# Moving the weight halves by 16 to 224 bytes in a partition, stage by stage

## The chip, the cores and the metric

The kernel runs on one core of a Trainium2 chip. The metric is the device time of one execution in microseconds. The times beside it come from repeated executions; the profile is of one further execution, taken by the hardware profiler. Lower is better.

## What is computed

The reference is a stack of transformer-like layers on 512 latent tokens (and, in the first layer, 256 context tokens) of width 1024, in fp32:

```python
for i in range(DEPTH):          # layer 0 "even", layer 1 "odd"
    x = x + gate1 * mixer(modulate(rms_norm(x, g1), shift1, scale1))
    x = x + gate2 * squared_relu_mlp(modulate(rms_norm(x, g2), shift2, scale2), w1, w2)
# mixer of layer 0: p = h @ w_in; a depthwise convolution of one half, differential attention
#   of the other, joined and multiplied by w_out
# mixer of layer 1: p = h @ w_in; long convolutions of one half, a gated delta rule of the other, w_out
# then two second layers: attention with latents and a gated recurrence beside it, both projected,
#   joined, multiplied by w_out, then a gated MLP (w_gate, w_up, w_down)
```

Most of the arithmetic is in the products `h @ w`. Everything else is norms, gates, convolutions, attention and scans between them.

## The kernel before

Each stage's products are run by one helper, `products` (lines 189 to 539). Activations stand with their features on the 128 partitions and tokens along the free axis. So that a product of fp32 numbers is precise in the chip's faster fp32r format, each operand is split into a **high half** (the fp32r rounding) and a **low half** (the rest), and each pair of blocks costs three matmuls: weight high by activation high, weight high by activation low, weight low by activation high (line 519 issues them all, in this order). The stationary operand, which TensorE loads ahead of each matmul, is a 128x128 block of a weight half; the moving operand is 512 latent tokens or 256 context tokens of an activation half. Three matmuls for each of the 128-row blocks of the weights add up in one PSUM bank. In jobs with `rows` the operands change places: a block of activations is stationary, and 512 columns of a weight half move. Jobs marked `native` are plain fp32 products without halves, and so are those of lines other than 519.

The weights of one unit (as a rule 8 blocks of 128 rows by 128 columns, or 4 by 256: 1024 numbers in each partition) pass through three stations:

- SP loads the unit from HBM into one of three or four buffers `raw`.
- VectorE makes the high half by a copy with a cast (`halve_weights`, line 356), into one of three buffers `high`.
- GpSimd makes the low half by a subtraction (`lower_weights`, line 450), into one of three buffers `low`.
- TensorE waits for the low half of the unit (line 450's semaphore) and issues its matmuls. A buffer of `high` and `low` comes free when the matmuls of the unit three before are done.

Buffers are stacked: each is allocated where the one before it ended, at the next multiple of 32 bytes in the partition. In `products` the order is `raw`, `low`, `high`, each of 12,288 bytes (16,384 for a `raw` of four). The halves of the activations were allocated by the caller before them. So the distance in a partition from an activation half to a weight half follows from the sizes of what lies between. All blocks of halves are multiples of 512 bytes apart, and all buffers between them are multiples of 512 bytes, with two exceptions:

- In the odd layer's input products the buffer `pads` (2 by 776 numbers, 6,208 bytes, that is 12 times 512 plus 64) lies between the halves and `raw`.
- In the second layers `lb`, `last`, `columns` and `marks` (32, 64, 96 and 48 bytes, the last one rounded up to 64: 256 together) lie between the part `work`, in which the halves named `x_high`, `ya_high` and `yb_high` are placed, and the halves of the normed input; after these come the weights.

In this text the **offset** of a stage is the distance from its activation halves to its weight halves, modulo 512 bytes. In the kernel before it is 0 in the even layer's four stages of products listed below, in the odd layer's output product and in its MLP; 64 in the odd layer's input products; and in the second layers 0 for the products of the normed input and the MLP's down product, and 256 for those of `x_high`, `ya_high`, `yb_high`.

The stages, in order of time, with the matmuls of halves in each:

| stage | function | matmuls of 512 columns | of 256 columns |
|---|---|---|---|
| even input | `even_mixer` | 528 | 384 |
| even output | `even_output` | 192 | 192 |
| even MLP | `squared_relu_mlp` (latent and context) | 1536 | 1536 |
| odd input | `odd_projections` | 696 | 216 |
| odd output | `odd_layer` | 192 | 0 |
| odd MLP | `squared_relu_mlp` (latent alone: `own_room`) | 1536 | 0 |
| second layers, each of two passes | `layer_products` | 2880 | 0 |

The counts follow from the strips of the jobs, 8 to 32 blocks of rows in each, and three matmuls for each block. In the second layers the first third of a stage has attention, scans and native products between the matmuls of halves; the later part (output, gate, up and down products) is almost nothing but them.

Of the kernel before, what the change touches and what calls it, by code (L numbers as in the profile page):

```python
# [188 lines left out]
def products(nc, m, jobs, ring_tiles=RING, beside=None, beside_scalar=None, signals=(), with_signals=None,  # L189
             before=None, loads=(), sides=(), banks=8, sums=None, settled=False):  # L190

# [69 lines left out]
    with ExitStack() as held:  # L261
        raw, low, high = held.enter_context(buffers(nc, raw=[P, R, 1024], low=([P, RH, 1024], F32R),
                                                    high=([P, RH, 1024], F32R)))
        block, *sems = held.enter_context(stage(
            nc, *[f"weights_loaded{r}" for r in range(R)], "high_ready", "low_ready", "accumulated",
# [1468 lines left out]
def squared_relu_mlp(nc, m, x, w1, w2, toks, scale, shift, gate, sides=()):  # L1734
# [5 lines left out]
    with ExitStack() as held:  # L1740
        *h, hid = held.enter_context(buffers(nc, **pair, hid=[P, FF1 // P, width]))
        room = held.enter_context(buffers(nc, **pair)) if own_room else h
        before = Norm(m, x, hid[:, 0:DC, :], hid[:, DC, :], DC, toks, D, scale, shift, halves=h, given=True)

        def relu(act, c, s, y):
            t0, tn = toks[s]
            return act.activation(hid[:, c, t0:t0 + tn], y, ACT.Relu)  # L1747

        def square(dve, c, s):
            t0, tn = toks[s]  # L1750
            return dve.tensor_tensor(hid[:, c, t0:t0 + tn], hid[:, c, t0:t0 + tn], hid[:, c, t0:t0 + tn], ALU.mult)  # L1751

        products(nc, m, [Job(w1, strip(0, FF1), h, toks, relu, "scalar", square),
                         Job(w2, FULL, hid, toks, residual(x, gate)(toks), "vector", written_by=0, room=room,
                             lead=6 if own_room else 1, room_after=None if own_room else 0)],
                 ring_tiles=3, before=before, sides=sides, sums=SquareSums(m, x, toks))

# [64 lines left out]
def even_mixer(nc, m, A, x, mods, small, gain, mix, q, k, v, written):  # L1822
# [4 lines left out]
    with ExitStack():  # L1827
        scale = lambda c, s: gain[:, c, s:s + 1]
        with ExitStack():
            w_in = A["ev_w_in"][0, :, :]  # L1830
            with ExitStack():
                with buffers(nc, conv=[P, 4, TG]) as conv:
                    with buffers(nc, pad=[P, 4, TG + GAP], odd_taps=[P, TG], flat=[P, 2, 512],
# [42 lines left out]
                        def convolve(dve, u, stored, signals):  # L1876
# [3 lines left out]
                            for c, n in steps[(u - 2) * per_unit:(u - 1) * per_unit] if 2 <= u <= last_unit else []:  # L1880
# [16 lines left out]
                                else:  # L1897
# [11 lines left out]
                                 beside=convolve, signals=("convolved",), with_signals=convolution_signals, before=before,  # L1909
                                 ring_tiles=3, banks=6, sides=[copies, Modulation(  # L1910
                                     m, A, [(0, n) for n in range(4, 12)],
# [15 lines left out]
def even_output(nc, m, A, x, mods, small, gain, mix):  # L1927
    toks = (LAT, CTX)
    shift = lambda which: (lambda c, s: mods[:, which * DC + c, s:s + 1])
    with buffers(nc, high=([P, DC, TA], F32R), low=([P, DC, TA], F32R)) as halves:  # L1930
        products(nc, m, [Job(A["ev_w_out"][0, :, :], FULL, mix, toks, residual(x, shift(2))(toks), "vector",
                             room=halves)],
                 ring_tiles=3, sides=[Gain(gain, mods, small.norm_g[:, 1, :], 4)], sums=SquareSums(m, x, toks))

# [797 lines left out]
def odd_layer(nc, m, A, x, mods, small, gain, spectra):  # L2732
# [5 lines left out]
    with buffers(nc, mix=[P, DC, T], u=[P, 12, T], gate=[P, 4, T]) as (mix, u, gate):  # L2738
# [9 lines left out]
        with buffers(nc, high=([P, DC, T], F32R), low=([P, DC, T], F32R)) as halves:  # L2748
            products(nc, m, [Job(A["od_w_out"][0, :, :], FULL, mix, (LAT,),
                                 residual(x, shift(2))((LAT,)), "vector", room=halves)],  # L2750
                     sides=[Gain(gain, mods, small.norm_g[:, 3, :], 4)], sums=SquareSums(m, x, (LAT,)))
    squared_relu_mlp(nc, m, x, A["mlp_w1"][1, :, :], A["mlp_w2"][1, :, :], (LAT,), scale, shift(3), shift(5))
# [57 lines left out]
def odd_projections(nc, m, w_in, halves, before, pads, short_w, short_b, conv_w, u, qk, v, gate, rest, squares, roots):  # L2810
# [45 lines left out]
    def convolve(dve, unit, stored, signals):  # L2856
# [16 lines left out]
        beside=convolve, signals=("convolved",), with_signals=with_signals, before=before,  # L2873
        ring_tiles=3, banks=7, sides=[delta])

# [945 lines left out]
def layer_products(nc, m, A, l, x, columns, halves, latent_halves, state_halves, x_halves, part, q, f, gate, i_rows,  # L3821
# [60 lines left out]
    def gated(dst, n):  # L3882
        def take(dve, c, s, y):
# [40 lines left out]
            written_by=15, room=halves, room_after=13, lead=6)],  # L3924
        before=before, ring_tiles=3, settled=True, sides=[constants, prep, attention, forget, levels, gates, states, norm], sums=SquareSums(m, x, toks))

# [121 lines left out]
```

How the kernel before makes its waits and increments, by code:

```python
    def __call__(self, ins):  # L54
        self.mark(ins)
        self.eng.wait_ge(self.sem, self.n)
# [6 lines left out]
    def wait(self, n=None):  # L63
        n = self.n if n is None else n
        if n > 0:
            self.eng.wait_ge(self.sem, n)
# [60 lines left out]
        @block.scalar  # L127
        def _(act):
            for dst, src in pairs[1::2]:
                act.dma_start(dst, src, allow_slow_non_contiguous=True).then_inc(arrived, 16)
            act.wait_ge(arrived, 16 * len(pairs))
# [2 lines left out]
def issue(eng, pairs, arrived):  # L135
    for dst, src in pairs:
        eng.dma_start(dst, src, allow_slow_non_contiguous=True).then_inc(arrived, 16)
    eng.wait_ge(arrived, 16 * len(pairs))
# [49 lines left out]
def products(nc, m, jobs, ring_tiles=RING, beside=None, beside_scalar=None, signals=(), with_signals=None,  # L189
# [127 lines left out]
        def stored(eng, j, c, part):  # L317
            p = index[j, c, part]
            if p in follow_at:
                eng.wait_ge(followed[follow_at[p][0]], follow_at[p][1])
            else:
                eng.wait_ge(taken[taken_at[p][0]], taken_at[p][1])
# [4 lines left out]
            j = len(jobs) - 1  # L327
            ended = {c: max(u for u, (i, cs, _, _) in enumerate(units) if i == j and c in cs)
                     for c in range(len(jobs[j].chunks))}
            first = min(c for c in ended if bank_of[index[j, c, 0]] == 0 and ended[c] >= len(units) - 4)
            sums.follow(raw, j, jobs[j].parts, ended, first, len(units),
                        lambda eng: eng.wait_ge(low_ready, halved(len(units) - 1)))
        @block.sync
```

## Time and profile before

| | |
|---|---|
| median of the runs shown | 3940.62 us (3938.89 to 3942.35) |
| span of the profiled execution, first to last instruction | 3934.4 us |
| TensorE matmuls, busy | 3645.1 us, 93% of the span, 18,494 instructions |
| TensorE weight loads, busy | 2932.7 us, 75% |
| VectorE, ScalarE, GpSimd, busy | 2035.1, 864.5, 1369.6 us |
| mean granted TensorE clock | 0.962 of full speed |

A time of an execution is some 5 to 8 us longer than the span, which begins with the first instruction and ends with the last; no separate time of the profiled execution is given. The recorded duration of a matmul holds its way through the array, so records overlap and "busy" counts the overlap once; the distance from one start to the next is what a matmul costs in a stream. In a timeline the first column is the start in us, the second the duration in us; "x16" means that 16 instructions of one form were merged into one line, and its duration runs to the end of the last. In a view of windows each engine has its busy time and the number of its instructions.

### The profile page before, as it was taken

The numbers are of one execution on the slowest core, as the hardware profiler recorded it, in microseconds if no ns is written. First come the engines' busy times: TensorE is split into PE (matmuls) and PEld (weight loads), VectorE is DVE, ScalarE is ACT, GpSimd is POOL, SyncE is SP. The second block draws the span as 40 slices with busy tenths as digits, with TensorE's granted clock in tenths as the row PEclk, the third lists the DMA queues.
The fourth block names the chain that finished last, engine by engine and source line by source line (L and its number), as shares of the span: only waits on it lengthen the run. The fifth ranks groups of instructions, "written<-read, shape, count | busy, mean of one in ns | idle before, by whom it ended". The sixth has DMA issues, their size and how long they took to land. (4 is left out here: it accounts for less than half of the span.)

```text
span 3934.4 us, 45661 instructions
## 1 busy us (share of the span) xinstructions
PE 3645.1 (93%) x18494; PEld 2932.7 (75%) x18494; DVE 2035.1 (52%) x3169; ACT 864.5 (22%) x1690; POOL 1369.6 (35%) x599
## 2 busy tenths in 40 slices
PE   6898988999989999968999899799999898899998
PEld 3684567888877889857888566688888576788887
DVE  5797643224446457673233367864243377853342
ACT  3213512110011233301100344422000344421001
POOL 2331043225554200005455222235455222245454
PEclk9898989999999999989999899999999999999999
DMA  5443312221113100112322232123332222223322
GB/s 171 150 150 134 129 43 75 60 64 59 61 53 91 51 1 1 51 45 73 98 94 91 61 81 53 50 67 100 97 92 80 82 61 54 52 78 96 97 91 80
DMA packets 400349, 306.78 MB, mean 78 GB/s; under 512 B 11228, under 2 KB 367782, under 8 KB 399559
## 3 DMA queue, kind: packets, MB, share of 16 engines
q1 hardware_dynamic: 398040, 303.37, 25.5%
q8 instruction: 149, 2.44, 0.3%
q10 hardware_dynamic: 2095, 0.44, 0.1%
q14 instruction: 65, 0.53, 0.0%
HBM read 297.48 MB, written 6.29 MB: 77 GB/s over the span
## 5 line engine op out<-in xcount | busy, mean ns | idle before, releaser
L450 POOL TENSOR_TENSOR low<-raw,high 128x1024 fp32r<-128x1024 f32 (+1 forms) x437 | 1049.5, 2402 | 2090.4 <-DVE high L356 2090.4
L519 PE MATMUL scores<-high 128*128 128x512 f32 (+1 forms) x1944 | 741.5, 381 | 72.0 <-DVE low L704 32.4
L519 PE MATMUL scores<-low,high 128*128 128x512 f32 (+1 forms) x1944 | 727.1, 374 | 0.0
L519 PE MATMUL scores<-high,low 128*128 128x512 f32 (+1 forms) x1944 | 726.3, 374 | 0.0
L356 DVE CAST high<-raw 128x1024 fp32r<-128x1024 f32 (+1 forms) x437 | 397.5, 910 | 499.6 <-PE scores L519 257.7
L519 PE MATMUL bank<-high 128*128 128x512 f32 (+1 forms) x1480 | 541.5, 366 | 0.2
L519 PE MATMUL bank<-low,high 128*128 128x512 f32 (+1 forms) x1480 | 538.8, 364 | 0.0
L519 PE MATMUL bank<-high,low 128*128 128x512 f32 (+1 forms) x1480 | 538.1, 364 | 0.0
L519 PEld LDWEIGHTS scores<-high 128*128 128x128 f32 x1944 | 375.5, 193 | 154.2 <-POOL low L450 53.9
L519 PEld LDWEIGHTS scores<-high,low 128*128 128x128 f32 x1944 | 374.6, 193 | 65.5
L519 PEld LDWEIGHTS scores<-low,high 128*128 128x128 f32 x1944 | 376.2, 194 | 61.7 <-issue 1.0
L519 PEld LDWEIGHTS bank<-high 128*128 128x128 f32 x1480 | 279.3, 189 | 49.3 <-issue 4.9
L519 PEld LDWEIGHTS bank<-high,low 128*128 128x128 f32 x1480 | 279.0, 189 | 45.1
L519 PEld LDWEIGHTS bank<-low,high 128*128 128x128 f32 x1480 | 279.3, 189 | 44.1 <-issue 0.5
L752 ACT ACTIVATE raw<-x_all 128x512 f32<-128x512 f32 (+1 forms) x48 | 32.4, 700 | 1070.3 <-POOL low L450 1013.7
L1751 DVE TENSOR_TENSOR hid<-hid 128x512 f32<-128x512 f32 x96 | 60.8, 633 | 328.5 <-ACT hid L1747 328.5
L519 PE MATMUL bank<-x_high,high 128*128 128x512 f32 x448 | 174.3, 389 | 0.0
L519 PE MATMUL bank<-x_low,high 128*128 128x512 f32 x448 | 174.3, 389 | 0.0
L519 PE MATMUL bank<-x_high,low 128*128 128x512 f32 x448 | 174.3, 389 | 0.0
L398 POOL TENSOR_TENSOR low<-hid,high 128x1536 fp32r<-128x1536 f32 (+1 forms) x23 | 103.7, 4509 | 132.7 <-DVE high L387 132.7
L519 PE MATMUL scores<-x_high,high 128*128 128x512 f32 x256 | 100.0, 391 | 0.0
L519 PE MATMUL scores<-x_high,low 128*128 128x512 f32 x256 | 99.6, 389 | 0.0
(632 smaller groups left out, 5260.2 us busy)
## 6 DMA issues: line engine op xcount, KB each, us to landing
raw<-in_mlp_w SPq DMA_DIRECT2D x128, 512.0 KB, 3.9
raw<-in_w_in SPq DMA_DIRECT2D x76, 512.0 KB, 3.9
ring<-in_ada_w SPq DMA_DIRECT2D x32, 1024.0 KB, 7.1
raw<-in_w_gate SPq DMA_DIRECT2D x44, 512.0 KB, 3.8
raw<-in_w_up SPq DMA_DIRECT2D x44, 512.0 KB, 3.8
raw<-in_w_down SPq DMA_DIRECT2D x40, 512.0 KB, 3.4
mix<-in_ada_w SPq DMA_DIRECT2D x16, 1024.0 KB, 6.3
raw<-in_od_w_in SPq DMA_DIRECT2D x29, 512.0 KB, 3.9
```

The costliest lines, as they stand in the source:

```text
L356: dve.tensor_copy(tile(high, u), tile(raw, u)).then_inc(high_ready, 1)
L398: return eng.tensor_tensor(low_, act, high, ALU.subtract)
L450: pool.tensor_tensor(tile(low, u), tile(raw, u), tile(high, u).bitcast(F32), ALU.subtract)\
L519: mm = pe.matmul(out(p), stationary, moving, start=(k0 + k == 0 and i == 0), stop=(k0 + k == job.kc - 1 and i == len(pairs) - 1))
L752: act.activation(self.tile(c), self.x[:, c, 0:self.width], ACT.Square).then_inc(self.squared, 1)
L1751: return dve.tensor_tensor(hid[:, c, t0:t0 + tn], hid[:, c, t0:t0 + tn], hid[:, c, t0:t0 + tn], ALU.mult)
```

## The change

`products` gets a parameter `skew`. `low` is allocated larger by that many 4-byte numbers and used from `skew` numbers on; `high`, which is allocated behind it, begins so much later too, rounded up to 32 bytes. No instruction is added or taken away, and `raw`, the activations and the order of the work stay as they are.

```diff
@@ products
-             before=None, loads=(), sides=(), banks=8, sums=None, settled=False):
+             before=None, loads=(), sides=(), banks=8, sums=None, settled=False, skew=0):
...
-        raw, low, high = held.enter_context(buffers(nc, raw=[P, R, 1024], low=([P, RH, 1024], F32R),
+        raw, low, high = held.enter_context(buffers(nc, raw=[P, R, 1024], low=([P, RH * 1024 + skew], F32R),
                                                     high=([P, RH, 1024], F32R)))
+        low = low[:, skew:].rearrange("p (r n) -> p r n", r=RH)
@@ squared_relu_mlp
-                 ring_tiles=3, before=before, sides=sides, sums=SquareSums(m, x, toks))
+                 ring_tiles=3, before=before, sides=sides, sums=SquareSums(m, x, toks), skew=32 if own_room else 4)
@@ even_mixer
-                                 ring_tiles=3, banks=6, sides=[copies, Modulation(
+                                 ring_tiles=3, banks=6, skew=48, sides=[copies, Modulation(
@@ even_output
-                 ring_tiles=3, sides=[Gain(gain, mods, small.norm_g[:, 1, :], 4)], sums=SquareSums(m, x, toks))
+                 ring_tiles=3, sides=[Gain(gain, mods, small.norm_g[:, 1, :], 4)], sums=SquareSums(m, x, toks), skew=56)
@@ odd_layer
-                     sides=[Gain(gain, mods, small.norm_g[:, 3, :], 4)], sums=SquareSums(m, x, (LAT,)))
+                     sides=[Gain(gain, mods, small.norm_g[:, 3, :], 4)], sums=SquareSums(m, x, (LAT,)), skew=12)
@@ odd_projections
-        ring_tiles=3, banks=7, sides=[delta])
+        ring_tiles=3, banks=7, skew=24, sides=[delta])
@@ layer_products
-        before=before, ring_tiles=3, settled=True, sides=[constants, prep, attention, forget, levels, gates, states, norm], sums=SquareSums(m, x, toks))
+        before=before, ring_tiles=3, settled=True, skew=24, sides=[constants, prep, attention, forget, levels, gates, states, norm], sums=SquareSums(m, x, toks))
```

The offsets become:

| stage | skew in bytes | offset before | offset after, of low / of high |
|---|---|---|---|
| even input | 192 | 0 | 192 |
| even output | 224 | 0 | 224 |
| even MLP | 16 | 0 | 16 / 32 |
| odd input | 96 | 64 | 160 |
| odd output | 48 | 0 | 48 / 64 |
| odd MLP | 128 | 0 | 128 |
| second layers | 96 | 0 and 256 | 96 and 352 |

## Rows read from the trace of the kernel before

**Rows 1.** The page, part 1: busy time (share of the span) and instructions.

```profile
PE 3645.1 (93%) x18494; PEld 2932.7 (75%) x18494; DVE 2035.1 (52%) x3169; ACT 864.5 (22%) x1690; POOL 1369.6 (35%) x599
```

**Rows 2.** Windows by stage, line 519 alone: window, length, PE, PEld, clock, DMA, GB/s.

```profile
121.70:321.60 199.90, 174.28 (x912) 147.99 (x912) 0.98 0.41 129
525.30:594.40 69.10, 68.97 (x384) 60.38 (x384) 0.97 0.12 39
605.40:1154.10 548.70, 541.42 (x3072) 475.89 (x3072) 0.99 0.20 59
1167.10:1371.00 203.90, 195.31 (x912) 158.20 (x912) 0.98 0.24 68
...
1820.70:2177.80 357.10, 354.46 (x1536) 291.71 (x1536) 0.98 0.30 90
2204.60:2590.00 385.40, 262.28 (x1016) 194.37 (x1016) 0.97 0.23 61
2590.00:3050.20 460.20, 442.09 (x1944) 364.42 (x1944) 1.00 0.29 88
```

**Rows 3.** Timeline of PE, odd MLP (offset 0): 55 matmuls, first and last.

```profile
1999.65 0.39 PE L519 MATMUL bank<-low,high 128*128 128x512 f32 x1
...
2011.89 0.39 PE L519 MATMUL scores<-low,high 128*128 128x512 f32 x1
```

**Rows 4.** Timeline of PE, even MLP (offset 0): ten matmuls of 256 columns, then 512.

```profile
1010.50 0.28 PE L519 MATMUL scores<-high,low 128*128 128x256 f32 x1
...
1011.70 0.40 PE L519 MATMUL bank<-high 128*128 128x512 f32 x1
1011.94 0.40 PE L519 MATMUL bank<-low,high 128*128 128x512 f32 x1
1012.17 0.39 PE L519 MATMUL bank<-high,low 128*128 128x512 f32 x1
1012.40 0.40 PE L519 MATMUL bank<-high 128*128 128x512 f32 x1
1012.63 0.39 PE L519 MATMUL bank<-low,high 128*128 128x512 f32 x1
1012.86 0.39 PE L519 MATMUL bank<-high,low 128*128 128x512 f32 x1
```

**Rows 5.** Timeline of PE, odd input (offset 64): 512 columns, ten matmuls in all.

```profile
1221.70 0.39 PE L519 MATMUL scores<-low,high 128*128 128x512 f32 x1
1221.93 0.40 PE L519 MATMUL scores<-high,low 128*128 128x512 f32 x1
1222.17 0.39 PE L519 MATMUL scores<-high 128*128 128x512 f32 x1
1222.40 0.40 PE L519 MATMUL scores<-low,high 128*128 128x512 f32 x1
...
1223.80 0.40 PE L519 MATMUL scores<-low,high 128*128 128x512 f32 x1
```

**Rows 6.** Timeline of PE, odd input (offset 64): 256 columns, thirteen matmuls, first and last.

```profile
1290.28 0.28 PE L519 MATMUL scores<-high,low 128*128 128x256 f32 x1
...
1291.64 0.28 PE L519 MATMUL scores<-high,low 128*128 128x256 f32 x1
```

**Rows 7.** Timeline of PE: native fp32 products of 512 columns, second layer.

```profile
2267.96 3.60 PE L519 MATMUL bank<-raw,work 128*128 128x512 f32 x8
2271.39 7.03 PE L519 MATMUL scores<-raw,work 128*128 128x512 f32 x16
```

**Rows 8.** Timeline of PE: halves, 512 columns, at half the granted clock; seven matmuls.

```profile
2205.63 0.63 PE L519 MATMUL scores<-high,low 128*128 128x512 f32 x1
...
2208.19 0.61 PE L519 MATMUL scores<-high,low 128*128 128x512 f32 x1
```

**Rows 9.** Groups by line, 2600 to 3040 us: the two engines that make the halves.

```profile
L450 POOL TENSOR_TENSOR low<-raw,high 128x1024 fp32r<-128x1024 f32 (+1 forms) x79 | 186.2, 2358 | 186.7 <-DVE high L356 186.7
...
L356 DVE CAST high<-raw 128x1024 fp32r<-128x1024 f32 (+1 forms) x79 | 68.5, 868 | 86.6 <-PE scores L519 50.8 <-PE bank L519 35.8
```

## The prediction

> **What bounds the kernel now.** I read the page's busy times first, then line 519 by windows of one stage each, then single starts in the timeline, and last the engines that feed TensorE. TensorE's matmuls are busy for 3645 of 3934 us [rows 1]. The windows show where: the products of halves fill their stages almost without a gap, 541 of 549 us in the even MLP, 354 of 357 in the odd MLP, 442 of 460 in the later part of a second layer; only in that layer's first part is line 519 busy for less, 262 of 385 us [rows 2]. The second pass of the second layers repeats the last two windows, with the same 1016 and 1944 instructions (80 of the 1016 are native passes, which leaves 936 matmuls of halves). So the time goes as the distance from one matmul's start to the next, and an edit matters as far as it changes that distance.
>
> The distance is the reading on which all else rests. In the odd MLP 54 steps take 12.24 us, 226.7 ns each [rows 3]. At the full clock of 2.4 GHz 512 columns are 213.3 ns, so 13.3 ns of each step are something else. In the even MLP the matmuls of 256 columns lie 120.0 ns apart (1.20 us for ten), again 13.3 ns over their 106.7 [rows 4]. The odd input stage runs the same instructions on the same shapes with the full clock, and its steps differ: 512 columns take 2.10 us for nine, 233.3 ns [rows 5], and 256 columns 1.36 us for twelve, 113.3 ns [rows 6]. The kernel's text names one thing in which this stage stands apart: its offset is 64 and not 0 or 256. So the offset matters, in both directions: it adds 6.7 ns to 512 columns and takes 6.7 ns from 256.
>
> Two more readings say what the extra is. Native fp32 products, which pass their columns at half the rate, lie 3.43 us / 8 = 428.8 ns apart [rows 7]; and halves at the half clock of 1.2 GHz lie 2.56 us / 6 = 426.7 ns apart, which is 512 columns and nothing more [rows 8]. Where the moving operand is read at half speed, the extra is 0 to 2.1 ns. It comes up when the moving read runs at its full rate beside the load of the next weights, and I take it for the two reads getting in each other's way in SBUF, which the offset shifts against each other. It also depends on when they start: after the 256-column matmuls the 512-column ones begin with steps of 240, 230, 230, 230 and 230 ns as printed [rows 4], longer than the 226.7 of a long run [rows 3]. The settled steps are 113.3, 120.0, 226.7 and 233.3 ns, all multiples of 6.67 ns. I expect other offsets to settle on this ladder too.
>
> **A rule on this.** The step of the same instruction on the same shape is 226.7 ns at offset 0 and 233.3 at 64 [rows 3, 5]. The Trainium skill, "TensorE: Matmul & The Clock Gate", section "Step-by-step: what each phase is for", says that TensorE reads SBUF through two independent ports and that loading the next weights takes no read bandwidth from the running matmul; "SBUF — State Buffer", section "SBUF: two separate sides", lets only VectorE and GpSimd contend on the engine side. By that rule an offset changes nothing and the time stays where it is; the trace disagrees by the 6.7 ns above. The same page on TensorE puts a warm step of 512 columns at 215.7 ns; if all steps fell to that, the sum would be about 130 us below the time before, an estimate from that page. No run here shows such a step for halves.
>
> **What the change removes, adds and moves.** It adds and removes no instruction, wait or transfer. It moves where three streams touch SBUF: VectorE's cast writes `high`, GpSimd's subtraction reads `high` and writes `low`, and TensorE reads both.
>
> *VectorE and GpSimd:* I cost them at nothing. A unit of 1024 weights feeds 24 matmuls of 512 columns, 24 x 226.7 ns = 5.44 us, while its cast takes 0.87 us and its subtraction 2.36 us [rows 9]. Both could take twice as long and the unit would still be ready in time; at 220 ns a step the unit takes 5.28 us, which changes nothing. The cover would go only if the subtraction took over 5.3 us.
>
> *TensorE, bounds.* The new offsets (192, 224, 16/32, 160, 48/64, 128, 96/352) stand in no row, so I bound the step. Below: 213.3 + 2.1 = 215.4 ns for 512 columns and 106.7 + 2.1 = 108.8 for 256, if the extra falls to that of the native products [rows 7]. Above: 512 columns at 240 ns, the longer of the two steps that alternate at offset 64 as they are printed, to 10 ns [rows 5], and 256 at 120 as now.
>
> *TensorE, what I take.* The value nearest to the rows is one rung of the ladder up, none, or one down, by stage. At offset 0 both reads begin in the same place of every 256 bytes; taking that away was worth a rung to 256 columns, whose whole length lies beside a load, and cost a rung at 64 to 512 columns. I let offsets that are no multiple of 64 go one rung down, 64-like ones behave as the odd input does, and 128 change nothing, being as symmetric as 0 and 256:
>
> - second layers, later part, two passes: 2 x 1944 x 6.67 ns = -25.9 us;
> - second layers, first part: 2 x 936 x 6.67 = 12.5; line 519 stands back behind other work there (262 of 385 us busy [rows 2]), so I let half of it arrive: -6.2;
> - even MLP: (1536 + 1536) x 6.67 = 20.5; its shift of 16 and 32 bytes is at most half the 64 of the odd input, so half: -10.2;
> - even output: (192 + 192) x 6.67 = -2.6;
> - odd input, leaving 64: 696 x 6.67 = -4.6, its 256 columns unchanged;
> - even input, 192 being 64 short of 256: +528 x 6.67 - 384 x 6.67 = +1.0;
> - odd MLP and odd output: 0.
>
> The sum is -48.5 us. For the profiled execution that is a span of 3934.4 - 48.5 = 3885.9; the median of the runs, 3940.6, is 6.2 us above that execution's span, and with it I forecast 3892 us, 1.2% less. Nothing new is late after that: GpSimd has half of each unit free, and DMA moves at 0.2 to 0.4 of its share in these windows [rows 2].
>
> **Rivals.**
>
> *The collisions go away almost everywhere.* Every stage settles at least one rung lower, at best at 215.4 and 108.8 ns. For: with the reads at half speed the extra is already gone, so it is no fixed cost [rows 7, 8]. Against: no settled step of halves in the trace is under 226.7 ns for 512 columns. One rung everywhere: 512 columns 2 x 1944 + 936 (half of the two first parts) + 1536 + 192 + 192 + 1536 + 696 + 528 = 9504, 256 columns 1536 + 192 + 384 = 2112; 11,616 x 6.67 ns = 77 us, 3863 us. At the lower bound: (9504 - 696) x 11.3 + 696 x 17.9 + 2112 x 11.2 + 216 x 4.5 ns = 137 us, 3804 us.
>
> *The new offsets are like 64, and the kernel gets slower.* The mechanism is the one seen in the odd input: away from 0, steps of 512 columns settle a rung higher and those of 256 a rung lower. For: it is the only offset other than 0 and 256 that the trace has, and 512 columns are four fifths of the matmuls. Against: one point says little of seven others. Price: (9504 - 696) x 6.67 - 2112 x 6.67 = +45 us, 3985 us. It decides as soon as the second layers go up, which hold half of these 512-column steps; with 240 ns everywhere and 256 columns unchanged it would be 8808 x 13.3 = +117, 4058 us.
>
> *Nothing happens.* Either the steps depend on something else that sets the odd input stage apart, or the gains and losses by stage cancel: 3941 us. For: 256 and 0 give the same step although they are different places. Against: rows 5 and 6 beside rows 3 and 4. That the change doesn't do what it says belongs here too: the offset would have to be undone by the allocation, and the sizes leave no room for that.
>
> **How the numbers follow.** I give the forecast (some stages a rung down, 3862 to 3925) 0.42, the collisions going away almost everywhere 0.23, nothing 0.15, slower 0.20. The predicted time is the forecast's, 3892 us. The range reaches from the lower bound of the second case to the price of the third, in round numbers 3805 to 3990 us. A measurement of this kernel tells about 2% (79 us) from no change: below 3862 lies nearly all of the second case and a part of the forecast, 0.30; above 4019 only the far end of the slower case, 0.07; the rest is 0.63.
>
> **What would show it.** In the timeline of the changed kernel the settled step of each stage tells: 220 ns in the second layers' later part and in the even output would show the forecast's main terms right, 226.7 would show that the offset doesn't matter there, 233 or more the slower rival. The odd input at 226.7 or less would show that 64 was its trouble. 226.7 in the odd MLP would show that 128 counts as 0. The number of instructions, the durations of the cast and the subtraction, and the DMA must be as before. I'm wrong if the second layers' step goes up, or if steps under 216 ns appear.

## The result and the profile after

The changed kernel takes 3990.12 us (median of 3989.98 and 3990.26) beside 3940.62 before: 1.0124 times as long, with an interval of 1.0095 to 1.0154. The forecast was 3892 us, 1.2% faster. The span of the profiled execution grew from 3934.4 to 3988.1 us, by 53.7. In every run for which both are given an execution takes 2.1 to 2.2 us more than its span (here 3990.26 and 3988.1), and not 5 to 8 as the section on the time before has it. So the profiled execution of before took some 3936.6 us, 4 us under its median, and the spans differ by more than the medians, which are 49.5 us apart. What came about is the second rival, "the new offsets are like 64, and the kernel gets slower", priced at 3985 us.

Page, part 1, of the kernel after, answering to [rows 1]:

```profile
PE 3705.6 (93%) x18494; PEld 2942.7 (74%) x18494; DVE 2031.9 (51%) x3169; ACT 864.1 (22%) x1690; POOL 1371.4 (34%) x599
```

Every count is the same, and VectorE, ScalarE and GpSimd are busy as long as before to within 4 us. TensorE's matmuls are busy for 60.5 us longer, its weight loads for 10.0.

Windows by stage of the kernel after, answering to [rows 2] with the same columns (the helper's line is 520 now):

```profile
122.50:323.10 200.60, 173.83 (x912) 146.40 (x912) 0.98 0.41 129
524.10:593.70 69.60, 69.50 (x384) 60.14 (x384) 0.97 0.13 38
605.10:1161.30 556.20, 548.04 (x3072) 475.90 (x3072) 0.99 0.19 58
1174.20:1379.40 205.20, 197.04 (x912) 160.23 (x912) 0.98 0.24 67
1774.10:1820.30 46.20, 46.20 (x192) 37.23 (x192) 0.96 0.16 49
1830.80:2195.50 364.70, 361.82 (x1536) 291.91 (x1536) 0.99 0.30 88
2221.50:2606.90 385.40, 265.09 (x1003) 193.43 (x1004) 0.96 0.23 60
2606.90:3085.90 479.00, 459.93 (x1958) 368.58 (x1956) 1.00 0.28 86
```

No stage became shorter. The even MLP went from 548.7 to 556.2 us, the odd MLP from 357.1 to 364.7; the last two windows, a whole pass of the second layers, from 845.6 to 864.4. The granted clock of each window is the one it had, to 0.01, and a weight load of line 519 or 520 lasts 0.19 us on average in both kernels: the growth is neither a lower clock nor a longer load.

The step, the distance between two starts, shows where it lies. First second layers, then odd MLP (answering to [rows 3]), in the timeline of PE of the kernel after:

```profile
2899.69 0.40 PE L520 MATMUL bank<-x_low,high 128*128 128x512 f32 x1
...
2904.14 0.40 PE L520 MATMUL bank<-x_high,low 128*128 128x512 f32 x1
...
1999.70 0.40 PE L520 MATMUL bank<-low,high 128*128 128x512 f32 x1
...
2004.82 0.40 PE L520 MATMUL bank<-high,low 128*128 128x512 f32 x1
```

The first two rows span 19 steps in 4.45 us, 234.2 ns each; the last two 22 steps in 5.12 us, 232.7 ns. In these rows the moving operand's half comes first, then the weights': "low,high" is the activations' low half by the weights' high one. Before, the odd MLP had 226.7 [rows 3], and so had the second layers, in the timeline of PE of the kernel before:

```profile
2899.27 0.39 PE L519 MATMUL bank<-x_low,high 128*128 128x512 f32 x1
...
2902.67 0.39 PE L519 MATMUL bank<-x_low,high 128*128 128x512 f32 x1
```

These are 15 steps in 3.40 us.

Two answers to [rows 8] and [rows 7], halves at half the clock and native products, in the timeline of PE of the kernel after:

```profile
2222.10 0.63 PE L520 MATMUL scores<-low,high 128*128 128x512 f32 x1
...
2224.23 0.63 PE L520 MATMUL scores<-high 128*128 128x512 f32 x1
...
2287.14 3.60 PE L520 MATMUL bank<-raw,work 128*128 128x512 f32 x8
```

Five steps in 2.13 us are 426 ns, as before. Over all steps of 512 columns at the half clock each stage of both kernels has a mean of 426.6 to 426.9 ns, so the distance shows in the step only at the full 2.4 GHz. Eight native products last 3.60 us, as before, but that says nothing of the distance: the change moved neither `raw` nor `work`. The engines that make the halves, groups from 2617 to 3057 us of the kernel after, answer to [rows 9]:

```profile
L451 POOL TENSOR_TENSOR low<-raw,high 128x1024 fp32r<-128x1024 f32 x76 | 182.4, 2401 | 196.6 <-DVE high L357 196.6
...
L357 DVE CAST high<-raw 128x1024 fp32r<-128x1024 f32 x76 | 68.0, 895 | 72.1 <-PE scores L520 42.1 <-PE bank L520 30.0
```

A unit's cast takes 0.90 us and its subtraction 2.40, of the 24 x 234.2 ns = 5.62 us in which TensorE uses the unit up: they stay covered.

By stage, from its first to its last matmul of halves; the steps are means over all that follow each other without a gap at the full clock, before and after:

| stage | us before, after | predicted, measured | step of 512 columns, ns | step of 256 columns, ns |
|---|---|---|---|---|
| even input | 199.5, 200.2 | +1.0, +0.7 | 227.8 to 230.3 | 119.7 to 116.7 |
| even output | 68.7, 69.2 | -2.6, +0.5 | 229.0 to 233.1 | 119.4 to 117.4 |
| even MLP | 548.3, 555.8 | -10.2, +7.5 | 228.4 to 232.9 | 119.5 to 119.0 |
| odd input | 203.5, 204.8 | -4.6, +1.3 | 233.3 to 233.3 | 113.6 to 119.9 |
| odd output | 45.0, 45.9 | 0, +0.9 | 226.7 to 231.2 | |
| odd MLP | 356.6, 364.4 | 0, +7.8 | 226.7 to 232.4 | |
| second layers, pass 1 | 845.1, 863.9 | -16.1, +18.8 | 227.2 to 234.2 | |
| second layers, pass 2 | 845.6, 864.3 | -16.1, +18.7 | 227.1 to 234.2 | |

The measured terms add up to +56.2 us, the span to +53.7; the stretches between the stages gave back 2.5.

### The profile page after: what moved, and what is told of

Same layout as the page of the kernel before. It is cut to its first block and busy times, and to the rows that moved or that the text cites. A ratio compares the mean times of both kernels' runs of the same rounds, so it can differ in the third digit from the quotient of the medians.

```text
span 3988.1 us, 45661 instructions
## 1 busy us (share of the span) xinstructions
PE 3705.6 (93%) x18494; PEld 2942.7 (74%) x18494; DVE 2031.9 (51%) x3169; ACT 864.1 (22%) x1690; POOL 1371.4 (34%) x599
## 5 line engine op out<-in xcount | busy, mean ns | idle before, releaser
L520 PE MATMUL scores<-high 128*128 128x512 f32 (+1 forms) x1944 | 751.1, 386 | 71.6 <-DVE low L705 30.8
L520 PE MATMUL scores<-low,high 128*128 128x512 f32 (+1 forms) x1944 | 737.1, 379 | 0.0
L520 PE MATMUL scores<-high,low 128*128 128x512 f32 (+1 forms) x1944 | 734.7, 378 | 0.0
L520 PE MATMUL bank<-high 128*128 128x512 f32 (+1 forms) x1480 | 547.2, 370 | 0.2
```

The source lines that it names most:

```text
L520: mm = pe.matmul(out(p), stationary, moving, start=(k0 + k == 0 and i == 0), stop=(k0 + k == job.kc - 1 and i == len(pairs) - 1))
```

## The experiments

All compute the whole of the reference. Diffs are against the changed kernel, shortened to the arguments and lines that differ, and "without `skew`" means that the argument is taken out. Where only one run was made, it is read by its stages, which say more here than its time; the time of the kernel before on the same chip stands beside each, since chips differ by some us.

**1. Everything at a distance of 0 or 256.** The even input and second layers get a distance of 256, the odd input 64 + 192 = 256. In the odd MLP and the two output products, activations and weights move together by 96 bytes; the even MLP is as before.

```diff
@@ squared_relu_mlp
+        if own_room:
+            held.enter_context(buffers(nc, gap=[P, 24]))
-  skew=32 if own_room else 4
@@ even_mixer, layer_products
-  skew=48
+  skew=64
...
-  skew=24
+  skew=64
@@ odd_projections
-  skew=24
+  skew=48
@@ even_output, odd_layer
-    with buffers(nc, high=
+    with buffers(nc, gap=[P, 24]), buffers(nc, high=
...
-  skew=56
...
-  skew=12
```

> Every stage has offset 0 or 256, but not the places of before: even input and second layers move their weights by 256 bytes, the odd input by 192 (offset 256 in place of 64), and in the even output, odd MLP and odd output activations and weights move together by 96 bytes. The even MLP is unchanged. Theory (the distance between weight halves and activation halves modulo 256 sets the step): 226.7 ns in all these stages, in the odd input too, where 512 columns fall from 233.3 to 226.7 (696 x 6.67 = -4.6 us) and 256 columns rise from 113.3 to 120 (216 x 6.67 = +1.4 us); the sum is 3937 us. Rival A (the place of the weights in the partition itself, or any move, sets it): the second layers at 230 to 235 ns and the odd MLP at 231 to 233, 3970 to 3995 us. Rival B (the engines that write the halves are slowed by a new place): the odd MLP as in the changed kernel, and longer casts or subtractions.

Measured: 3932.36 us (median of 10) beside 3935.53 (13), a ratio of 0.9994 with an interval of 0.9984 to 1.0003. In the timeline of PE of this kernel, odd input (answering to [rows 5]), then odd MLP:

```profile
1221.71 0.39 PE L520 MATMUL scores<-high 128*128 128x512 f32 x1
...
1225.79 0.39 PE L520 MATMUL scores<-high 128*128 128x512 f32 x1
...
1999.75 0.39 PE L520 MATMUL bank<-low,high 128*128 128x512 f32 x1
...
2003.15 0.39 PE L520 MATMUL scores<-low,high 128*128 128x512 f32 x1
```

Eighteen steps in 4.08 us and fifteen in 3.40 are 226.7 ns each. So the odd input was not a stage with slow products: it had a bad distance, and at 256 its 512 columns fall from 233.3 to 227.2 on average, its 256 columns rise from 113.6 to 119.7, and the stage takes 200.8 us, not 203.5. In the odd MLP, moving both operands together by 96 bytes changed nothing. With the parameter still there and the distances at 0 or 256, the whole growth is gone. In the places tried it is the distance of the two that counts, modulo 256, and not the place of either.

**2. The low weight halves alone.** They begin where the change puts them; the high halves stay where they were modulo 256, at 64 in the odd input and at 0 elsewhere. The even MLP is as before.

```diff
@@ products
+        room = skew + (-skew) % 64
-  low=([P, RH * 1024 + skew], F32R)
+  low=([P, RH * 1024 + room], F32R)
-        low = low[:, skew:].rearrange("p (r n) -> p r n", r=RH)
+        low = low[:, skew:skew + RH * 1024].rearrange("p (r n) -> p r n", r=RH)
@@ squared_relu_mlp
-  skew=32 if own_room else 4
+  skew=32 if own_room else 0
```

> Only the low weight halves move, by the amounts of the change; the high halves begin at offset 0 again (64 and 0 as before in the odd input's case: it moves by 256), and the even MLP is as before. Theory (the loads of the weights meet the moving reads): two loads of three stay aligned, so the settled sequence is broken but less often disturbed: second layers between 228 and 233 ns, odd MLP likewise, 3950 to 3980 us. Rival A (the place of the high halves alone decides): 226.7 ns, 3940 us. Rival B (GpSimd's writing of the low halves at the new place is what costs): the whole price of the change without the even MLP's 7 us, 234 ns in the second layers, 3982 us.

Measured: 3976.84 us (before on this chip 3935.53). The second layers take 859.2 and 860.1 us at a mean step of 232.5 ns, the odd MLP 361.9 at 231.1. The timeline of PE of this kernel, odd MLP:

```profile
2000.14 0.39 PE L521 MATMUL bank<-high 128*128 128x512 f32 x1
2000.37 0.40 PE L521 MATMUL bank<-low,high 128*128 128x512 f32 x1
2000.60 0.40 PE L521 MATMUL bank<-high,low 128*128 128x512 f32 x1
2000.84 0.39 PE L521 MATMUL bank<-high 128*128 128x512 f32 x1
2001.06 0.40 PE L521 MATMUL bank<-low,high 128*128 128x512 f32 x1
...
2003.61 0.39 PE L521 MATMUL bank<-high 128*128 128x512 f32 x1
```

Fifteen steps in 3.47 us, 231.3 ns: a triple of unequal steps that repeats. Averaged over the stage, the step after "high" is 226.7 ns, that after "low,high" 232.5, that after "high,low" 234.2. Only the last two have the moved low weights beside them: the second while they are loaded for the next matmul, the third while the matmul itself uses them. Here two thirds of the steps carry the whole loss. The second layers of the same run, with the low weights at 96, don't follow that: the step after "high", which has no moved weights beside it, is the longest there, 233.2 ns, that after "low,high" 231.7 and that after "high,low" 232.6. Moving one weight half alone doesn't help in either, and a single step isn't explained by the operands beside it alone.

**3 and 4. Other distances.** Each stage gets another skew, so that a distance is seen in more than one stage (the numbers of the diffs are of 4 bytes).

```diff
@@ even_mixer: skew
-  48
+  16, and 8 in the fourth
@@ even_output
-  56
+  32, and 40
@@ squared_relu_mlp, odd and even
-  32 and 4
+  16 and 16, and 48 and 8
@@ odd_projections
-  24
+  8, and 56
@@ odd_layer
-  12
+  24, and 8
@@ layer_products
-  24
+  8, and 40
```

> Other offsets by stage: even input 64, even output 128, even MLP 64, odd input 96, odd output 96, odd MLP 64, second layers 32. Theory (the offset modulo 256 alone decides, whatever the stage): odd MLP 233.3 ns as the odd input had at 64, even MLP 512 columns at 233 and 256 columns at 113.3, odd input at 96 the 234 ns that the second layers had there; the second layers at 32 are unknown, 227 to 236. Sum for 230 ns at 32: 3975 us. Rival A (each stage has its own best place, by what lies around it): the odd MLP at 64 differs from 233.3 by over 2 ns, and the even MLP's 256 columns stay at 119 to 120.

> Even input 32, even output 160, even MLP 32 for both halves, odd input 32 (288), odd output 32, odd MLP 192, second layers 160. Theory (offset alone): the second layers at 160 show the odd input's 233.3 ns of the changed kernel, the odd output and input at 32 the step of the second layers in the run with 32 there, the odd MLP at 192 near the even input's 230 or above; no stage under 226.7 ns, 3975 to 4000 us. Rival (a better place exists): one of the offsets 32, 160, 192 gives 220 ns or less for 512 columns; in the second layers that would be 3905 us or less.

Measured: 3974.29 and 3976.83 us (before on this chip 3935.53). The timeline of PE of the third kernel: even MLP at 64, 256 columns and then 512, and odd MLP at 64.

```profile
699.86 0.28 PE L520 MATMUL bank<-high 128*128 128x256 f32 x1
...
700.54 0.39 PE L520 MATMUL bank<-high 128*128 128x512 f32 x1
...
2000.07 0.39 PE L520 MATMUL bank<-high 128*128 128x512 f32 x1
...
2003.57 0.39 PE L520 MATMUL bank<-high 128*128 128x512 f32 x1
```

Six steps of 256 columns in 0.68 us are 113.3 ns, and fifteen of 512 in 3.50 us are 233.3: what [rows 6] and [rows 5] showed of 64 in the odd input, now in two other stages. The stage is no cause; the distance is. And in the fourth kernel's odd MLP, at 192, in its timeline of PE:

```profile
1999.61 0.39 PE L520 MATMUL bank<-low,high 128*128 128x512 f32 x1
...
2003.73 0.39 PE L520 MATMUL bank<-low,high 128*128 128x512 f32 x1
```

Eighteen steps in 4.12 us, 228.9 ns, under the 230 that was expected from the even input (why is told below the table of distances), the least away from 0 in these two kernels. None comes below 226.7. As a whole the even MLP at 64 was no longer than before, 547.7 us beside 548.3 to 549.6 in the runs that left it at 0: what its 512 columns lost, its 256 columns gave back.

**5 and 6. Small distances.** Both weight halves get 64 numbers more room and are used from `skew` on, so that distances of a few bytes can be set.

```diff
@@ products
+        low_room = (RH * 1024 + 64 if skew else RH * 1024)
-  low=([P, RH * 1024 + skew], F32R), high=([P, RH, 1024], F32R)
+  low=([P, low_room], F32R), high=([P, low_room], F32R)
-        low = low[:, skew:].rearrange("p (r n) -> p r n", r=RH)
+        low, high = (t[:, skew:skew + RH * 1024].rearrange("p (r n) -> p r n", r=RH) for t in (low, high))
```

> Offsets of few bytes to either side of 0 (both weight halves at the same one): even input 248, even output 252, odd input 240, odd output 8, odd MLP 4, second layers 16; even MLP unchanged. Theory (the two reads of TensorE meet, and 0 is a place where the sequence settles at 226.7): the step rises off 0 as it did at 32, to between 228 and 235 ns; 3950 to 3985 us. Rival (0 is an accident of a grid of 32 bytes, and a better place lies a few bytes off): 220 ns or less in the second layers at 16 or in the odd MLP at 4, 3905 us or less. Third possibility (lines of 16 bytes or more are read whole, so that less than a line makes no difference): 226.7 at 4, 8, 248 and 252.

> The same with other amounts: even input 240, even output 232, odd input 112, odd output 24, odd MLP 16, second layers 8. Theory: the odd MLP at 16 repeats the second layers of the run beside it within 1 ns, the even input at 240 its odd input; the second layers at 8 lie between 226.7 and the step at 16; 3945 to 3985 us. Rival (a better place a few bytes off): 220 ns or less somewhere.

Measured: 3954.22 and 3953.92 us (before on this chip 3939.88). Four bytes are enough: the odd MLP went from 226.7 to 232.4 ns. That rules out the third possibility, by which less than 16 bytes would change nothing. The expectation that one distance gives one step fell at 16 bytes: 229.1 ns on average in the second layers of the fifth kernel, 233.3 in the odd MLP of the sixth. The timeline of PE of the fifth kernel, second layers, shows why:

```profile
2699.67 0.39 PE L521 MATMUL bank<-high,low 128*128 128x512 f32 x1
...
2702.47 0.39 PE L521 MATMUL scores<-x_high,low 128*128 128x512 f32 x1
...
2799.62 0.39 PE L521 MATMUL bank<-x_low,high 128*128 128x512 f32 x1
...
2803.02 0.39 PE L521 MATMUL scores<-x_low,high 128*128 128x512 f32 x1
```

Twelve steps in 2.80 us are 233.3 ns; 97 us later, in the same stage and at the same distance, fifteen in 3.40 are 226.7. Taken by streaks without a gap, of at least a dozen steps, 3443 of the 5426 steps lie in streaks with a mean of 227 ns, 1807 in streaks of 233, and 176, all in the job with `rows`, between. A streak keeps its level until it is interrupted. So 16 bytes have two settled levels, and the distance alone doesn't decide which is taken; the mean of a stage hides that.

All distances, with the mean step in ns (of several stages where there are two numbers; the stages of 512 columns alone give the cleaner ones):

| bytes, modulo 256 | 512 columns | 256 columns |
|---|---|---|
| 0 | 226.7 to 229.0 | 119.4 to 119.7 |
| 4, 8 | 232.4, 230.7 | |
| 16 | 229.1 (of streaks at 227 and 233) and 233.3 | |
| 24, 32 | 231.1, 233.0 to 233.3 | 118.3 to 118.7 (at 32) |
| 64 | 232.1 to 233.3 | 113.5 to 113.7 |
| 96, 112 | 234.2, 233.3 | 117.5, 119.8 |
| 128 | 232.4 to 233.5 | 118.2 |
| 160 | 233.2 to 233.4 | 119.9 to 120.1 |
| 192 | 228.9 to 230.3 | 116.7 |
| 224, 232 | 233.1, 231.1 | 117.4, 118.4 |
| 240, 248, 252 | 227.5 to 230.5, 233.1, 233.3 | 118.2 to 119.2, 117.8, 120.0 |

The even input's means of 512 columns mix two kinds of job. In its last 144 matmuls, a job with `rows`, the weights move and the activations are stationary, so the distance from the moving operand to the stationary one is the offset with the other sign: 64 where the table says 192, and 192 where it says 64. The timeline of PE shows it: the changed kernel (192), first an ordinary job, then the one with `rows`, and the latter in the third kernel (64):

```profile
148.04 0.39 PE L520 MATMUL bank<-high 128*128 128x512 f32 x1
...
153.31 0.39 PE L520 MATMUL bank<-high,low 128*128 128x512 f32 x1
...
293.99 0.40 PE L520 MATMUL scores<-high,low 128*128 128x512 f32 x1
...
301.69 0.39 PE L520 MATMUL scores<-high,low 128*128 128x512 f32 x1
...
292.69 0.39 PE L520 MATMUL scores<-high 128*128 128x512 f32 x1
...
297.73 0.39 PE L520 MATMUL scores<-low,high 128*128 128x512 f32 x1
```

These are 23 steps in 5.27 us, 229.1 ns; 33 in 7.70, 233.3; and 22 in 5.04, 229.1. So at 192 and 64 the step goes by the distance from the moving to the stationary operand, with its sign: the ordinary jobs have the 228.9 of the odd MLP at 192, the job with `rows` the 233.3 of 64. At 16 and 240 the mirror fails: with an offset of 240 the ordinary jobs have 228.3, within 1 ns of the odd input's 227.5 as expected, but the job with `rows` 236.4, which is no level of 16, and the second layers' job with `rows` at 16 has 231.2 to 231.8.

**7. Each length at its better place.** 512 columns are shortest at 0 and 256 columns at 64, so the context tokens' halves get buffers of their own, 64 bytes further from the weights than a multiple of 256, while the latent ones are at 0 (or 256). This is done in the even input, the first product of the even MLP and the odd input; all else is without `skew`.

```diff
+class Apart:
+    def __init__(self, latent, context):
+        self.latent, self.context = latent, context
+    def __getitem__(self, key):
+        p, c, t = key
+        return self.context[p, c, t.start - T:t.stop - T] if t.start >= T else self.latent[p, c, t]
+APART = dict(context_high=([P, DC, TC], F32R), context_low=([P, DC, TC], F32R), gap=[P, 16],
+             latent_high=([P, DC, T], F32R), latent_low=([P, DC, T], F32R))
...
@@ odd_projections
-  skew=24
+  skew=48
```

> The weights stay at offset 0 to the latent tokens' activations, and in three stages the context tokens' activations alone are put 64 bytes off: their halves get buffers of their own, 64 bytes ahead of the place that would be 0 (even input, the first job of the even MLP, odd input). The odd input's weights move by 192 bytes, so that its 512 columns come to 256. Everything else is at the places of before. Theory (each matmul's step follows from the distance of its moving operand to the weights that are loaded beside it): 512 columns stay at 227 to 229 ns, and 256 columns fall from 120 to 113.3 in the even input (384 x 6.3 = -2.4 us) and the even MLP's first half (768 x 6.2 = -4.7 us) and stay at 113.3 in the odd input, whose 512 columns fall to 227 (-4.2 us): -11 us together, ratio 0.997. Rival (a stage has one state for all its columns, and a 64 in it spoils the settled sequence of 512): 512 columns at 230 to 233 ns in these stages, and the sum no better than before, ratio 1.000 or above.

Measured: 3930.94 us (median of 11) beside 3939.39 (15) for the kernel before, a ratio of 0.998 with an interval of 0.9971 to 0.9989: a small gain, but over both kernels. The timeline of PE of this kernel, even MLP, from 256 to 512 columns:

```profile
699.72 0.28 PE L520 MATMUL bank<-context_high,low 128*128 128x256 f32 x1
...
700.90 0.39 PE L520 MATMUL bank<-latent_high,high 128*128 128x512 f32 x1
701.13 0.39 PE L520 MATMUL bank<-latent_low,high 128*128 128x512 f32 x1
701.35 0.39 PE L520 MATMUL bank<-latent_high,low 128*128 128x512 f32 x1
...
703.85 0.39 PE L520 MATMUL bank<-latent_low,high 128*128 128x512 f32 x1
```

Ten steps of 256 columns take 1.18 us, 118.0 ns, and thirteen of 512 take 2.95, 226.9. The even input takes 198.9 us (199.5 before), the even MLP 547.2 (548.3), the odd input 200.4 (203.5); 3.1 of these 4.8 us are the odd input's, whose 512 columns leave 64. The rest of the 8.4 us between the medians is not located; these two traces are of different chips. The 256 columns came to 118 and not to the 113.3 that I had expected from experiment 3: I had taken 64 to set their step by itself, and it doesn't where both distances are in one stage. The rival, by which the 64 would have spoilt the 512 columns, didn't come about either: they stay at 226.9. The cause of the 118 stays open, and by the stages 4.8 us came of the 11 that were expected. The second product of the even MLP and the even output were not taken apart.

**8. The second layers undone.** The changed kernel, without `skew` in the second layers alone.

```diff
@@ layer_products
-  skew=24
```

> The changed kernel with the second layers' weights back at their place of before; the other stages keep the change. Theory (the price is a sum of independent stages, and the second layers hold most of it): their two passes go back from 864 to 845.5 us each, 3990 - 37 = 3953 us, with the other stages' steps as in the changed kernel. Rival (the price comes from somewhere else and is only seen there): more than 10 us away from 3953.

Measured: 3958.89 us (before on this chip 3939.39). The passes are back at 846.0 and 846.2 us. The other stages of the table above sum to +18.7, which makes 3958.1: the terms of the stages add. One step is not as in the changed kernel, though. In the odd output, where the two kernels are the same, the timeline of PE shows the changed kernel's first and then this one's:

```profile
1777.64 0.40 PE L520 MATMUL scores<-high,low 128*128 128x512 f32 x1
...
1819.94 0.40 PE L520 MATMUL bank<-high,low 128*128 128x512 f32 x1
...
1780.88 0.39 PE L520 MATMUL scores<-high,low 128*128 128x512 f32 x1
...
1823.57 0.40 PE L520 MATMUL bank<-high,low 128*128 128x512 f32 x1
```

183 steps without a gap take 42.30 and 42.69 us, 231.2 and 233.3 ns. So 16 bytes are not the only distance with more than one level: at 48 and 64 the same code kept one of two in two executions.

**9. One activation half, or one weight half, moved.** In the odd MLP the low activation halves alone are moved, by 128 bytes; in the second layers the high weight halves alone, by 128; in the odd output the low activation halves by 64; all else is without `skew`.

```diff
@@ products
-        low = low[:, skew:].rearrange("p (r n) -> p r n", r=RH)
+        low = low[:, 0:RH * 1024].rearrange("p (r n) -> p r n", r=RH)
@@ squared_relu_mlp
+        if own_room:
+            pair = dict(high=pair["high"], gap=[P, 32], low=pair["low"], rest=[P, 32])
...
+            h, room = h[0::2], room[0::2]
@@ odd_layer
-        with buffers(nc, high=([P, DC, T], F32R), low=([P, DC, T], F32R)) as halves:
+        with buffers(nc, high=([P, DC, T], F32R), gap=[P, 16], low=([P, DC, T], F32R), rest=[P, 48]) as (*halves,):
+            halves = halves[0::2]
@@ layer_products
-  skew=24
+  skew=32
```

> Each group of three matmuls is: first, weight high by activation high, with the next load a weight high; second, weight high by activation low, with the next load a weight low; third, weight low by activation high, with the next load a weight high. In the odd MLP the low halves of the activations alone move by 128 bytes (odd output: by 64), the weights stay. In the second layers the high halves of the weights alone move by 128 bytes. Theory (a moving read meets the load of the next weights): in the odd MLP only the second matmul has a moving operand off the load beside it, exactly as where the low weights had moved alone by 128; so the same three steps are expected, 227, 232.5 and 234 ns, with a sum of 693 to 694 ns for three. In the second layers the first and the third are off and the second is not: the second alone is short, and the sum for three is another one, 693 to 703 ns. Rival (a matmul's distance to its own weights, loaded before, decides): the second matmul alone is slow in the odd MLP and the third is at 226.7, a sum of 686 ns; and in the second layers the first and the second are slow and the third is short. Time 3955 to 3970 us.

Measured: 3976.66 us (before on this chip 3937.48), above the range that was expected. In the odd MLP of this kernel, in its timeline of PE:

```profile
1999.99 0.40 PE L520 MATMUL bank<-high 128*128 128x512 f32 x1
...
2003.46 0.39 PE L520 MATMUL bank<-high 128*128 128x512 f32 x1
```

Fifteen steps in 3.47 us, the sum for three that experiment 2 had (693.3 ns over the whole stage beside 693.4), though only one matmul in three reads the moved half. The single steps did not come out as expected: 230.8, 229.6 and 232.9 ns by kind, in a sequence that repeats over more than three. In the second layers they are 232.4, 232.5 and 234.6, where the second was to stay short, and the odd output's mean is 232.0. Steps of one kind differ within such a sequence, so a step depends on the steps ahead of it, too, and this run can't tell whether the moving read meets the load of its own weights or of the next ones. That stays open. In the odd MLP of this run the weight halves are where they were before, and so are the writes of VectorE and GpSimd to them. The step rose all the same, from 226.7 to 231.1 on average: it isn't the place of those writes that costs.

## Why the prediction was wrong

- **The distance sets the step, and both lengths feel it:** right, and the base of everything. Experiment 1 shows it (the same stages at 0 and at 256), experiment 3 confirms the odd input's reading in two other stages. The alternative that something else sets the odd input apart is gone. The distance doesn't fix the step alone: at 16, and at 48 and 64, a stream keeps one of two levels (experiments 5 and 8), and 256 columns at 64 had 118 beside 512 columns at 0 (experiment 7).
- **The failed step** is "I let offsets that are no multiple of 64 go one rung down". It carried -25.9, -6.2, -10.2, -2.6 and -4.6 us, all of the gain. There was a row for 0 and one for 64, and the sign for all else was chosen by an argument about symmetry that no row bore. The runs put 512 columns above 226.7 ns on average at every distance tried but 0 and 256 (240 comes nearest, 227.5 beside 227.2 at 256 in the odd input). For 512 columns no distance tried was a gain: before the change, six of seven stages already stood at the best one found. For 256 columns a rung down was seen at 64 alone, 113.5 to 113.7 ns in whole stages beside 116.7 to 120.1 at the other distances.
- **"128 change nothing"** failed in the same way: 226.7 became 232.4 in the odd MLP, +7.8 us where 0 stood. 128 is no second 0. The odd output was put at 0 too, though by the prediction's own words its 48 and 64 should have gone a rung down or behaved as 64; it went from 226.7 to 231.2, +0.9 us.
- **The ladder** held in part. At 32, 64 and 160 the mean step is 233.3, one rung of 6.67 ns up. Elsewhere the mean lies between or above (228.9 at 192, 234.2 at 96). Most of these means, some of 233.3 among them, are of repeating sequences of unequal steps, as in experiment 2, and not of one settled step.
- **The even input** was the one term that took its sign from the row of 64: +1.0, measured +0.7. That the size came out is luck: its 512 columns rose by 2.5 ns and its 256 columns fell by 3.0 on average, where 6.67 was forecast for both, and the two nearly cancel either way.
- **The odd input** was to gain 4.6 us from its 512 columns leaving 64, "its 256 columns unchanged". The 512 columns stayed at 233.3 at 160, and the 216 of 256 columns rose from 113.6 to 119.9: 216 x 6.3 ns = 1.4 us, the whole of its +1.3.
- **VectorE and GpSimd at nothing**, and half-clock steps untouched: right. The native steps could tell nothing, as their operands weren't moved.
- **Half of the first part of the second layers arrives:** too little. Cut at the same matmul, the 937th of halves, the first parts of the two passes grew by 4.7 and 4.5 us and the later ones by 14.1 each. 9.2 us of at most 2 x 936 x 7.0 = 13.1 are about seven tenths.
- **The slower rival** had the sign of the 512 columns right at every distance, and came near in size: +45 priced, +49.5 measured. That it came so near is in part luck, as its parts missed both ways: the second layers were 32.2 of it and cost 37.5; the even MLP was 0, its 256 columns paying for its 512, and cost 7.5, since at 16 and 32 bytes the 256 columns fell by 0.5 ns only; the odd MLP was 10.2 and cost 7.8.
- **That nothing would change**, which the prediction drew from the Trainium skill's two independent read ports ("TensorE: Matmul & The Clock Gate", section "Step-by-step: what each phase is for"), is not what these runs show for halves at the full clock: experiment 3 against experiment 1 is 233.3 beside 226.7 ns in the odd MLP, with the same instructions. Whether the ports themselves are at fault no run shows.

That the two reads of TensorE get in each other's way remains an inference. It fits that the extra vanishes at the half clock and that the distance sets it; no view shows the reads themselves. The rival that TensorE is slowed by what VectorE and GpSimd write fits less well: they are busy for 0.90 and 2.40 of the 5.62 us of a unit, and a streak keeps its step, or its repeating sequence, through all of it.

## What to carry to other kernels

Read the distance between two starts, not the busy share, when a stream of matmuls fills a stage: here 226.7 and 233.3 ns are the same instructions, 3% apart, on engines that look equally busy. Where streams of 512 columns run in this format at the full clock, keep the moving operand and the weights a multiple of 256 bytes apart in the partition (a small buffer in between with an odd size was enough to lose it), and look at the step of each stage after any change of the allocation. A sign taken from one known point is not a trend: with a row at 0 and one at 64, the row's own sign is the likelier guess for the rest.

## What the runs showed of the hardware that was not expected

- Four bytes of distance cost 5.7 ns a step (226.7 to 232.4), nearly what 64 cost, 6.6.
- At 16 bytes there are two settled levels, 226.7 and 233.3 ns, and a stream keeps the one it has fallen into until it is interrupted. The odd output, at 48 and 64, ran its 183 steps at 231.2 ns in one execution and at 233.3 in another.
- At 64 and 192 the distance counts with its sign, from the moving operand to the stationary one: 233.3 and 229.1 ns, and the other way round where the two operands change places.
